# Delta rule: two chains half a level apart on TensorE, and one head of four with its inverse in its own partition half

## The reference

```
T     = (I + strictly_lower(diag(beta) K K^T))^-1            # per tile, 128 x 128
v_new = (T weighted by decays) (beta v - beta exp(cum) K S)
out   = (q exp(cum)) S + (decayed scores q K^T) v_new
S     = chunk_decay * S + (K exp(rest))^T v_new
```

## Time and profile before

| what | value |
|---|---|
| median of 3 runs | 3143.7 us (3142.03 to 3144.26) |
| the profiled execution | time 3148.52 us, span 3146.7 us, granted clock 0.959 |
| TensorE busy over the span | 2877.9 us, 91% |
| VectorE busy | 1179.2 us, 37% |
| ScalarE, GpSimd busy | 671.0 us, 295.6 us |
| the delta rule's iterations | 1466.93 to 1812.47 us of the span |

### The profile page before, as it was taken

The page is one execution under the profiler, slowest core; times in us unless marked ns, Lnnn a source line. Parts: engine busy times, 40 slices in busy tenths (PEclk is TensorE's granted clock), DMA queues, the critical chain, the costliest instruction groups (busy, mean ns, idle before and its releaser), DMA issues. The chain is left out here.

```text
span 3146.7 us, 42886 instructions
## 1 busy us (share of the span) xinstructions
PE 2877.9 (91%) x18239; PEld 1669.1 (53%) x18239; DVE 1179.2 (37%) x2252; ACT 671.0 (21%) x1529; POOL 295.6 (9%) x383
## 2 busy tenths in 40 slices
PE   6999998999898899998999979799999699999998
PEld 3344574446577455557898834565444444444443
DVE  1052461096344169834666655441012311111111
ACT  2111341111233155413333214331001100000000
POOL 0000020000001000002666500100000000000000
PEclk9999999998897999999999999899999799999999
DMA  8431013142000421001011142104210399999998
GB/s 270 160 134 54 1 34 120 42 100 62 1 1 34 139 81 52 29 12 45 30 37 33 33 149 81 54 1 174 101 56 25 131 427 426 427 427 427 427 427 360
DMA packets 136561, 442.23 MB, mean 141 GB/s; under 512 B 29634, under 2 KB 41351, under 8 KB 108590
## 3 DMA queue, kind: packets, MB, share of 16 engines
q1 hardware_dynamic: 136370, 439.48, 36.2%
HBM read 428.70 MB, written 10.76 MB: 140 GB/s over the span
## 5 line engine op out<-in xcount | busy, mean ns | idle before, releaser
L333 PE MATMUL banks<-weight_ring,rows_turned 128*128 128x512 f32 (+1 forms) x1576 | 680.7, 592 | 30.8 <-DMA weight_ring<-in_w_in 14.8
L333 PEld LDWEIGHTS banks<-weight_ring,rows_turned 128*128 128x128 f32 x1576 | 300.4, 196 | 403.8 <-issue 390.4
L2410 PE MATMUL banks<-rows_turned,weight_ring 128*128 128x256 f32 (+1 forms) x768 | 252.7, 489 | 1.6 <-PEq L1363 1.3
L2410 PEld LDWEIGHTS banks<-rows_turned,weight_ring 128*128 128x128 f32 x768 | 147.1, 192 | 100.5 <-issue 85.7
L3894 PE MATMUL banks<-weight_ring,chosen_turned 128*64 128x512 f32 (+1 forms) x696 | 174.5, 558 | 10.2 <-DMA weight_ring<-in_w_up 6.5
L3894 PE MATMUL banks<-expert_weights_early,chosen_turned 128*64 128x512 f32 (+1 forms) x672 | 169.3, 558 | 11.6 <-DMA expert_weights_early<-in_w_up 8.0
L1431 PE MATMUL banks<-weight_ring,mix_turned 128*128 128x512 f32 x320 | 138.8, 594 | 4.1 <-ACT mix_turned L1444 2.1
L3996 DVE TENSOR_TENSOR hidden<-hidden,banks 128x512 f32<-128x512 f32 (+1 forms) x24 | 14.0, 639 | 325.9 <-PE banks L3894 325.9
L333 PE MATMUL banks<-weight_ring,branch_turned 128*128 128x512 f32 x256 | 112.8, 594 | 1.9 <-PE banks L333 1.1
L3894 PEld LDWEIGHTS banks<-weight_ring,chosen_turned 128*64 128x64 f32 x696 | 62.3, 137 | 97.8 <-issue 94.4
L3894 PEld LDWEIGHTS banks<-expert_weights_early,chosen_turned 128*64 128x64 f32 x672 | 60.7, 137 | 95.3 <-issue 91.7
(11 more groups left out here) (589 smaller groups left out, 4618.0 us busy)
## 6 DMA issues: line engine op xcount, KB each, us to landing
weight_ring<-in_w_gate SPq DMA_DIRECT2D x29, 1408.0 KB, 17.2
weight_ring<-in_w_up SPq DMA_DIRECT2D x29, 1408.0 KB, 15.2
expert_weights_early<-in_w_gate SPq DMA_DIRECT2D x28, 1408.0 KB, 18.9
expert_weights_early<-in_w_up SPq DMA_DIRECT2D x28, 1408.0 KB, 16.4
expert_weights_early<-in_w_down SPq DMA_DIRECT2D x36, 1024.0 KB, 17.0
weight_ring<-in_w_down SPq DMA_DIRECT2D x35, 1024.0 KB, 17.5
weight_ring<-in_l_w_in SPq DMA_DIRECT2D x15, 2048.0 KB, 8.5
weight_ring<-in_w_in SPq DMA_DIRECT2D x13, 2048.0 KB, 7.9
```

Of the source, the lines that this page charges most:

```text
L333: ins = kit.nc.tensor.matmul(self.bank(u), lhsT, rhs, start=(k == 0), stop=(k == nk - 1))
L2410: ins = nc.tensor.matmul(kit.ps[:, bank(u), 0:n], w[:, k, f * P:(f + 1) * P], hT[:, k, h0:h0 + n], start=(k == 0), stop=(k == KD - 1))
```

## The change

Nothing is computed that was not computed before; what moves is order and place.

TensorE's list: z of left at level i is issued together with both updates of right at level i - 1, head by head, and z of right at level i with both updates of left at level i (`update_and_level`). Level 0 of left stands alone, and so does the last update of right (`update_alone`). Each such pair begins with the waits of both (`level_begin`, `update_begin`), and z now also waits for the chain's last `inverse` update. Solve of left moves from after the second pair of level 1 to between its two pairs.

Place: head 3 of each chain no longer crosses; its z is summed in its own partition half (`beside`), its `turned` update stays there too. The sums get new columns: z and turned in pieces of 64 columns, 192 apart, over the first two banks of a chain (head 3 in the second bank), the start of the inverse beside them, inverse updates in the second half of the second bank. In off, head 3 crosses instead. Cross comes in two pieces per chain: heads 0 to 2, then head 3 after a wait for the first piece.

Other engines: ScalarE copies z as 128 x 256 also for off, and does new values of left between the copies of left and right in level 1 and those of right likewise in level 2. VectorE does `turned` and `inverse` of left, then residual, then both of right, then state; the last inverse update is whole instead of half.

```diff
@@ -2526,7 +2526,8 @@
         sig = lambda n, c: kit.counter(f"{n}_{hg}", c)
         self.keys_summed, self.base_ready, self.off_ready, self.solver_ready = (sig(n, N) for n in ("keys_summed", "base_ready", "off_ready", "solver_ready"))
         self.masked, self.dt_summed = sig("masked", 5 * N), sig("dt_summed", 5 * N)
-        self.z_summed, self.z_ready, self.d_summed = (sig(n, 6 * N) for n in ("z_summed", "z_ready", "d_summed"))
+        self.d_summed = sig("d_summed", 7 * N)
+        self.z_summed, self.z_ready = (sig(n, 6 * N) for n in ("z_summed", "z_ready"))
...
-        self.flat = lambda b: kit.ps[:, 4 * hg + b, :]
         self.low = lambda b: kit.ps[:, 4 * hg + b, 0:256].rearrange("p (h n) -> p h n", h=4)
-        self.high = lambda b: kit.ps[:, 4 * hg + b, 256:512].rearrange("p (h n) -> p h n", h=4)
+        two = kit.ps[:, 4 * hg:4 * hg + 2, :].rearrange("p b n -> p (b n)")
+        slots = two[:, 0:768].rearrange("p (h s) -> p h s", h=4)
+        self.level_sums, self.base_sums = slots[:, :, 0:CHUNK], slots[:, :, CHUNK:2 * CHUNK]
+        self.level_and_base = slots[:, :, 0:2 * CHUNK].rearrange("p h (j n) -> p h j n", j=2)
+        self.inverse_sums = two[:, 768:1024].rearrange("p (h n) -> p h n", h=4)
+        self.keys_sums = two[:, 0:384].rearrange("p (a s) -> p a s", a=2)[:, :, CHUNK:3 * CHUNK].rearrange("p a (b n) -> p a b n", b=2)
...
-            def level(c, b, i):
-                n = 5 * b + i
-                pe.wait_ge(c.masked.sem, c.masked(n + 1))
+            def beside(h, o_rows):
+                return o_rows if h == 3 else HALVES[1 - HALVES.index(o_rows)]
+
+            def level_begin(c, b, i):
+                pe.wait_ge(c.masked.sem, c.masked(5 * b + i + 1))
                 pe.wait_ge(c.turned_ready.sem, c.turned_ready(7 * b + 2 + i))
+                if i:
+                    pe.wait_ge(c.inverse_ready.sem, c.inverse_ready(5 * b + i))
+                elif b:
+                    pe.wait_ge(c.solver_ready.sem, c.solver_ready(b))
+
+            def level_head(c, b, i, h):
                 mask = c.odd if i % 2 else c.even
-                for h in range(4):
-                    for o_rows, other in (HALVES, HALVES[::-1]):
-                        ins = nc.tensor.matmul(c.low(0)[other, h, :], mask[o_rows, h, :], c.turned[o_rows, h, :], start=True, stop=True, tile_position=(o_rows.start, other.start))
-                        if i == 0:
-                            ins = nc.tensor.matmul(c.high(0)[other, h, :], c.turned[o_rows, h, :], kit.part("ident_half")[o_rows], start=True, stop=True, tile_position=(o_rows.start, other.start))
-                ins.then_inc(c.z_summed.sem, 1)
-
-            def update(c, b, i):
+                for o_rows in HALVES:
+                    p = beside(h, o_rows)
+                    ins = nc.tensor.matmul(c.level_sums[p, h, :], mask[o_rows, h, :], c.turned[o_rows, h, :], start=True, stop=True, tile_position=(o_rows.start, p.start))
+                    if i == 0:
+                        ins = nc.tensor.matmul(c.base_sums[p, h, :], c.turned[o_rows, h, :], kit.part("ident_half")[o_rows], start=True, stop=True, tile_position=(o_rows.start, p.start))
+                if h == 3:
+                    ins.then_inc(c.z_summed.sem, 1)
+
+            def update_begin(c, b, i):
                 pe.wait_ge(c.z_ready.sem, c.z_ready(6 * b + i + 1))
                 if i:
                     pe.wait_ge(c.inverse_ready.sem, c.inverse_ready(5 * b + i))
-                if b and i == 0:
-                    pe.wait_ge(c.solver_ready.sem, c.solver_ready(b))
-                first, later = in_order(batches[b][0])
+
+            def turned_head(c, b, i, h):
+                for o_rows in HALVES:
+                    p = beside(h, o_rows)
+                    ins = nc.tensor.matmul(c.level_sums[o_rows, h, :], c.inverse[p, h, :], c.z[p, h, :], start=True, stop=True, tile_position=(p.start, o_rows.start))
+                if h == 3:
+                    ins.then_inc(c.dt_summed.sem, 1)
+
+            def inverse_head(c, b, i, h):
+                for p in HALVES:
+                    ins = nc.tensor.matmul(c.inverse_sums[p, h, :], c.z[p, h, :], c.inverse[p, h, :], start=True, stop=True, tile_position=(p.start, p.start))
+                if h == 3:
+                    ins.then_inc(c.d_summed.sem, 1)
+
+            def update_alone(c, b, i):
                 for h in range(4):
-                    for o_rows, other in (HALVES, HALVES[::-1]):
-                        turned = nc.tensor.matmul(c.low(0)[other, h, :], c.inverse[o_rows, h, :], c.z[o_rows, h, :], start=True, stop=True, tile_position=(o_rows.start, other.start))
-                    for o_rows in HALVES if i < 4 else (later,):
-                        ins = nc.tensor.matmul(c.low(1)[o_rows, h, :], c.z[o_rows, h, :], c.inverse[o_rows, h, :], start=True, stop=True, tile_position=(o_rows.start, o_rows.start))
-                turned.then_inc(c.dt_summed.sem, 1)
-                ins.then_inc(c.d_summed.sem, 1)
-
-            def off(c, b):
-                first, later = in_order(batches[b][0])
+                    inverse_head(c, b, i, h)
+                    turned_head(c, b, i, h)
+
+            def update_and_level(c, b, i, other, b2, i2):
+                for h in range(3):
+                    level_head(other, b2, i2, h)
+                    inverse_head(c, b, i, h)
+                turned_head(c, b, i, 0)
+                level_head(other, b2, i2, 3)
+                turned_head(c, b, i, 1)
+                inverse_head(c, b, i, 3)
+                turned_head(c, b, i, 2)
+                turned_head(c, b, i, 3)
+
+            def off_begin(c, b):
                 pe.wait_ge(c.off_ready.sem, c.off_ready(b + 1))
                 pe.wait_ge(c.turned_ready.sem, c.turned_ready(7 * b + 7))
-                for h in range(4):
-                    ins = nc.tensor.matmul(c.low(0)[later, h, :], c.matrix_off[later, h, :], c.turned[later, h, :], start=True, stop=True, tile_position=(later.start, later.start))
-                ins.then_inc(c.z_summed.sem, 1)
-
-            def cross(c, b):
+                pe.wait_ge(c.inverse_ready.sem, c.inverse_ready(5 * b + 5))
+
+            def off_head(c, b, h):
                 first, later = in_order(batches[b][0])
-                pe.wait_ge(c.z_ready.sem, c.z_ready(6 * b + 6))
-                pe.wait_ge(c.inverse_ready.sem, c.inverse_ready(5 * b + 5))
-                for h in range(4):
-                    ins = nc.tensor.matmul(c.low(1)[first, h, :], c.inverse[later, h, :], c.z[later, h, :], start=True, stop=True, tile_position=(later.start, first.start))
+                p = beside(h, first)
+                ins = nc.tensor.matmul(c.level_sums[p, h, :], c.matrix_off[later, h, :], c.turned[later, h, :], start=True, stop=True, tile_position=(later.start, p.start))
+                if h == 3:
+                    ins.then_inc(c.z_summed.sem, 1)
+
+            def cross(c, b, heads):
+                first, later = in_order(batches[b][0])
+                if 3 in heads:
+                    pe.wait_ge(c.d_summed.sem, c.d_summed(7 * b + 6))
+                else:
+                    pe.wait_ge(c.z_ready.sem, c.z_ready(6 * b + 6))
+                for h in heads:
+                    p = beside(h, first)
+                    ins = nc.tensor.matmul(c.inverse_sums[first, h, :], c.inverse[p, h, :], c.z[p, h, :], start=True, stop=True, tile_position=(p.start, first.start))
                 ins.then_inc(c.d_summed.sem, 1)
 
...
                 for i in range(5):
-                    for c in chains:
-                        level(c, it, i)
+                    level_begin(left, it, i)
+                    if i:
+                        update_begin(right, it, i - 1)
+                        update_and_level(right, it, i - 1, left, it, i)
+                    else:
+                        for h in range(4):
+                            level_head(left, it, 0, h)
                     if stating and i == 0:
                         seen(left, it - 1)
+                    if stating and i == 1:
+                        solve(left, it - 1)
                     if stating and i == 2:
                         solve(right, it - 1)
                     if stating and i == 3:
                         outer(left, it - 1)
                     if stating and i == 4:
                         outer(right, it - 1)
-                    for c in chains:
-                        update(c, it, i)
+                    level_begin(right, it, i)
+                    update_begin(left, it, i)
+                    update_and_level(left, it, i, right, it, i)
                     if stating and i == 0:
                         seen(right, it - 1)
-                    if stating and i == 1:
-                        solve(left, it - 1)
                     if stating and i == 2:
                         output(left, it - 1)
                     if stating and i == 3:
                         output(right, it - 1)
```

(53 more changed lines are left out.)

16 lines of the change are left out of this document (8 added, 8 removed).

## The result

| us | before | after |
|---|---|---|
| median of the runs | 3143.98 (3142.03 to 3149.34, 4 runs) | 3166.33 (3162.99 to 3172.49, 4 runs) |
| profiled execution: time, span | 3148.52, 3146.7 | 3168.02, 3166.2 |
| delta stage in it, first keys to the last output sum added | 345.5 | 365.2 |
| of that with TensorE at its 1.2 GHz level | 10.2, in 3 stretches | 51.2, in 11 |

The kernel became slower: ratio 1.0067, 95% interval 1.0053 to 1.0082. That is 22 us, and the time is outside the forecast range. The profiled stage grew by 19.7 us and the span by 19.5, so everything happened in the stage that the change touches.

What follows compares the result with a forecast made beforehand. The prediction took the delta stage to be bound by TensorE's in-order queue with short holes; packing gains and bare half levels nearly cancelled, iteration terms summing to +1.4 us, so 3145 us, range 3135 to 3158.

Steps and rivals of the forecast that it cites:

- the clock: Low clock in iterations 1, 2 and 8, estimated at 1.2 us each, taken away because later keys shorten the hole.
- laid-out sum of +1.4: Delta stage, all iterations: gains and losses add to +1.4 us, largest term iteration 0 at +4.5.
- Rival (b): Clock falls in iteration 0 and keeps falling in 1, 2, 8: +9 us, 3153; chance 0.20.
- The chain: Half level without state work: 0.70 issue, VectorE's two updates, way back; at least 1.92 us, idle for 1.2.
- way back: From VectorE's second update to TensorE's next pair: taken as 0.20 us, bounds 0.04 and 0.25.
- strided reads at nothing: VectorE and ScalarE reading sums in pieces 192 apart: costed at 0; at 0.30 more each, +24 us.
- rival (c): Pairs of two chains don't run side by side (+12) or strided reads cost (up to +24): 3157 to 3169; chance 0.08.
- The -2.2 us of iterations 9 and 10 together: Iterations ending on VectorE, which reaches its state update earlier: 29.4 us for 30.6 and 30.5, -2.2 for both.
- the 10.3 us of the earlier trace: Read as TensorE's longest wait in the stage, for VectorE's matrix step (L3021) at the start of an iteration.
- Rival (a): TensorE stays the bound everywhere and the packing is earned: -7.5 us, 3136; chance 0.17.

Runs made afterwards that it cites:

- e9: Changed kernel with one wide unread matmul (512 or 384 columns) per half level without state work, two of 128 in the tail: 3153.20 us, ratio 1.0030.
- e11: Changed kernel with wide unread matmuls in the holes and the inverse waits of z and off diagonal z only before head 3: 3143.18 us, ratio 0.9992.
- e13: Kernel before with two wide unread sums of 128 columns in each iteration's tail: 3142.49 us, ratio 0.9985.
- e12: Changed kernel with the wide unread matmuls in iteration 0 only: 3161.67 us, ratio 1.0052.
- e7: Kernel before with one edit, z of the next level also waits for the chain's inverse update: 3150.65 us, ratio 1.0023.
- e3: Changed kernel with all engines back in the old order, keeping the new places and the early inverse wait: 3156.28 us, ratio 1.0034.
- e4: Changed kernel with z's wait for the inverse moved to before head 3 only: 3145.05 us, ratio 1.0001.
- e10: Changed kernel with z's inverse wait only before head 3, plus wide unread matmuls in bare halves and tail: 3143.00 us, ratio 0.9995.
- e1: Changed kernel with many unread 64x64 matmuls in half levels without state work and in the tail: 3170.11 us, ratio 1.0073.

## Why the prediction was wrong

**The sum of what happened**, from the stages of the profiles: the clock in the changed kernel 365.2 - 351.8 = 13.4 (after against e9); the early waits for the inverse 351.8 - 341.3 = 10.5 (e9 against e11, about 4 us of it standing still that e11 has not); the order and the places by themselves, filling included, 341.3 - 341.7 = -0.4 (e11 against e13); and the kernel before had 345.5 - 341.7 = 3.8 of low clock itself, which the sum must not count twice. 13.4 + 10.5 - 0.4 - 3.8 = 19.7. The ratios of the table (their differences times the 3146 us of the kernel before) give the sum with other terms: 11.6 for the clock, 12.0 for the waits, +2.2 for order and places, -4.7 for the kernel before, 21.1 in all. So a term is good to 2 or 3 us, and the sign of the third is not known. The fillings cost something too, which makes the price of the clock a little low.

**The step that failed is the clock.** I took the three falls of the kernel before away, about 3.6 us, because the keys come later and the hole ahead of left z gets shorter, and I counted none for the new kernel. It had eleven, the first of them 17 us long: 13.4 us of time. Against a laid-out sum of +1.4 the stage grew by 19.7; 13.4 of the 18.3 in between are this. The price of one fall was about right (1.2 us by the earlier trace rows; 3.8 for three in e13, 0.9 each in e12). The number of them was wrong. I looked at one hole, that ahead of left z, and not at the new ones in the tail: the last right update alone, then off and cross with their waits, and keys behind them at the low clock. A hole alone doesn't make a fall, though: e7 has the holes of the earlier trace rows and eleven new ones of 0.9 us, and none; e3 has its two rows of new waits, and one. What decides between them no run here shows. Rival (b) named the mechanism, but held it to iteration 0 and to the three iterations that already had it: 3153. Its iteration 0 was right (+4 forecast, 30.3 against e9's 25.9 measured); iterations 4 to 7, 9, 10 and the last were left out. The Trainium skill ("TensorE: Matmul & The Clock Gate", A second HAM failure mode) describes, for another kernel, short idle times between groups of matmuls that make the clock swing; the windows after the change (0.93 to 0.95 in nine iterations, 0.72 in iteration 0) agree with it; e7 and e3 show that such holes needn't do it.

**The chain was right, nearly to the end.** Pairs in 0.71 us for 0.70, updates 0.42 and 0.41, way back 0.21 for 0.20, a half level 1.96 to 2.00 for 1.92, strided reads at nothing: L3079 and L3083 have means of 421 and 415 ns over 110 each, which with the 0.71 excludes rival (c). e9 has no falls and can be held against the layout: 25.9, 26.3, 27.7 for 25.2, 26.5, 27.5 in iterations 0 to 2; 29.4, 29.3, 28.9 for 29.2 in 3 to 5; 28.2 for 27.85 in 6. It is longer by 1.0, 1.3, 0.4 and 1.2 in 7 to 10, where TensorE stands still for 1.16, 1.27 + 0.33, 0.58 and 1.00 us in its profile. These stops, 4.7 us of e9, are most of the rest of the error (351.8 - 345.5 = 6.3 for 1.4, so 4.9); I had no term for them. In the changed kernel itself, iteration 3 keeps its clock: 30.4, less the stop of 1.27, is 29.1 for the forecast 29.2.

**The -2.2 us of iterations 9 and 10 together** did not come (30.7 and 30.4 us, where the kernel before took 30.6 and 30.5): as the tail above shows for 9, VectorE was early as forecast and TensorE's slow keys took it back. With an even clock and no stops in them the gain is there: 29.1 and 29.1 in e11, for the forecast 29.4.

**One reading was wrong, without effect on the sum:** the 10.3 us of the earlier trace rows are the total of seven waits, the longest 2.0, and not one wait.

**Rival (a)** needed half a level under 1.75 us. The early wait rules it out, and e4 shows what it held back: 21 us. Part of that is the clock, whose low time fell from 51.2 to 23.9 us with the shorter holes. I had put the wait into the chain and never asked whether all four heads needed it. Even without it the layout does not get measurably below the kernel before (e4, e10, e11).

**Open:** what makes the clock fall after some holes and not after others; what makes TensorE stand still inside a group, and whether it does so in the same places in each execution. That it comes with more matmuls shows in e1; fewer with the same order were not tried.

## What to carry to other kernels

When a change cuts one long queue into short groups with waits between, count the new holes over the whole loop, tail and head too, and price the clock for each of them with what one existing fall costs in the profile. That is an upper bound, since many holes here cost no fall; a few cheap wide matmuls in the holes test it in one run. A wait needed by one part of a group belongs ahead of that part, put last, provided the consumer doesn't need that part first. Compare layouts at an even clock, or a gain and a loss of the clock will pass for one of the layout.

## What the hardware showed beyond that

Filling with many small matmuls and with one wide one are not the same. 1420 more records of 64x64 took most of the low clock away (51.2 to 10.2 us), but TensorE stood still in 23 places, 17.3 us in all, and nothing was gained; one matmul of 384 or 512 columns per hole had 4.7 us of it. Work that nobody reads made the tuned kernel before faster: 3.8 us of the stage, 0.15% of the time. And the same holes of up to 2.0 us came with three falls of the clock in the kernel before and with none in the profile of e7.
